# The second mixer's probability-times-value matmuls and its fold, each one pipeline step sooner

## The reference

```python
def mixer_b(h, w_in, q_gain, k_gain, cos, sin):
    z = h @ w_in                                    # three groups of q, k, v, and a gate
    for g, (window, dilation) in enumerate(((128, 1), (512, 4), (2048, 16))):
        q, k, v = ...                               # 16 query heads, 4 key heads
        q = partial_rope(rmsnorm(q, q_gain[g]), cos, sin)
        k = partial_rope(rmsnorm(k, k_gain[g]), cos, sin)
        o, lse = dilated_group(q, k, v, window, dilation)   # banded attention, keys by stride
        outs.append(o); lses.append(lse)
    wts = jax.nn.softmax(jnp.stack(lses), axis=0)   # weight of each group's result
    o = jnp.einsum('gbsh,gbshd->bshd', wts, jnp.stack(outs))
    return o.reshape(b, s, BRANCH_WIDTH) * jax.nn.silu(gate)
```

## Time and profile before

| | us |
|---|---|
| median of 3 runs | 3348.26 (3345.35 to 3348.67) |
| the profiled execution | 3348.16 |
| its span | 3346.4 |
| PE busy | 3249.7 (97%) |
| DVE busy | 2053.1 (61%) |
| ACT busy | 1642.5 (49%) |
| POOL busy | 1394.3 (42%) |

### The profile page before, as it was taken

One profiled execution on the slowest core, in us unless ns is written; L12 is line 12 of the kernel. 1 busy time (PEld: TensorE's weight loads), 2 busy tenths in 40 slices (PEclk: granted clock), 3 DMA queues, 4 the chain that ended last, 5 costly groups with the idle time before them and its releaser, 6 DMA issues. The chain is left out here.

```text
span 3346.4 us, 58949 instructions
## 1 busy us (share of the span) xinstructions
PE 3249.7 (97%) x19285; PEld 2778.4 (83%) x19285; DVE 2053.1 (61%) x4209; ACT 1642.5 (49%) x3846; POOL 1394.3 (42%) x1778
## 2 busy tenths in 40 slices
PE   8999999999999989999999999999999899999999
PEld 7887788999999977779998778888887778888887
DVE  7456773455666675548887665665347866565335
ACT  3567216667667761436665643333235743333333
POOL 6465534555667754223334344443003244443000
PEclk9999999999999989999999999999999899999999
DMA  8211772111222235200001222222464112222464
GB/s 301 80 34 47 283 272 100 47 45 51 67 67 73 76 134 188 88 26 1 0 0 51 108 76 77 91 76 91 147 222 145 68 70 81 76 91 83 147 199 162
DMA packets 111991, 338.36 MB, mean 101 GB/s; under 512 B 11794, under 2 KB 40386, under 8 KB 102979
## 3 DMA queue, kind: packets, MB, share of 16 engines
q1 hardware_dynamic: 111810, 336.12, 29.0%
HBM read 274.18 MB, written 61.10 MB: 100 GB/s over the span
## 5 line engine op out<-in xcount | busy, mean ns | idle before, releaser
L2205 PE MATMUL ps<-down_high,hidden_high 128*128 128x512 f32 x688 | 268.1, 390 | 1.1 <-DVE hidden_low L2063 0.5
L2206 PE MATMUL ps<-down_low,hidden_high 128*128 128x512 f32 x688 | 267.7, 389 | 0.0
L2207 PE MATMUL ps<-down_high,hidden_low 128*128 128x512 f32 x688 | 267.7, 389 | 0.0
L2061 DVE TENSOR_TENSOR down_low<-down_raw,down_high 128x1024 fp32r<-128x1024 f32 x86 | 108.7, 1263 | 252.1 <-ACT down_high L1970 252.0
L2141 PE MATMUL ps<-columns_combined,up_high_even 128*128 128x512 f32 (+1 forms) x648 | 247.6, 382 | 12.4 <-DVE columns_combined L4250 2.7
L2143 PE MATMUL ps<-columns_combined,up_low_even 128*128 128x512 f32 (+1 forms) x648 | 246.3, 380 | 0.0
L2142 PE MATMUL ps<-columns_combined,up_high_even 128*128 128x512 f32 (+1 forms) x648 | 246.2, 380 | 0.0
L2141 PE MATMUL ps<-columns_combined,up_high_odd 128*128 128x512 f32 x616 | 239.8, 389 | 5.4 <-DVE gates L2069 5.4
L2142 PE MATMUL ps<-columns_combined,up_high_odd 128*128 128x512 f32 x616 | 239.6, 389 | 0.0
L2143 PE MATMUL ps<-columns_combined,up_low_odd 128*128 128x512 f32 x616 | 239.6, 389 | 0.0
L1151 ACT ACTIVATE masked_then_probs<-masked_then_probs,unit_rows 128x256 f32<-128x256 f32 (+1 forms) x512 | 229.1, 450 | 21.5 <-DVE sink_term L1239 20.2
(11 more groups left out here) (473 smaller groups left out, 9777.4 us busy)
## 6 DMA issues: line engine op xcount, KB each, us to landing
mod_weights<-in_w_mod SPq DMA_DIRECT2D x48, 1024.0 KB, 6.7
up_raw<-in_w_up SPq DMA_DIRECT2D x44, 1024.0 KB, 4.8
down_raw<-in_w_down SPq DMA_DIRECT2D x88, 512.0 KB, 3.6
hidden_columns<-hidden SPq DMA_DIRECT2D x44, 512.0 KB, 2.6
hidden_columns<-hidden_columns SPq DMA_DIRECT2D x88, 256.0 KB, 3.9
w_unit_raw<-in_w_in_b SPq DMA_DIRECT2D x22, 768.0 KB, 4.4
x_kept<-x SPq DMA_DIRECT2D x24, 512.0 KB, 2.8
group_rows<-unit_rows SPq DMA_DIRECT2D x64, 132.0 KB, 1.8
```

What stands on the lines that cost most here:

```text
L2205: nc.tensor.matmul(out, h_hi[to][:, t], down_hi[to][:, cols], start=begin, stop=False)
L2206: nc.tensor.matmul(out, h_hi[to][:, t], down_lo[to][:, cols], start=False, stop=False)
L2207: last = nc.tensor.matmul(out, h_lo[to][:, t], down_hi[to][:, cols], start=False, stop=(end and to == self.slot(h, f, s)))
```

## The change

For the second mixer, out moves from step i+6 to i+5 and fold from i+7 to i+6; the first mixer keeps both. `DEPTH_` follows (6 steps of drain, not 7), and so do `FILLING` (5, not 6) and one wait of PE before it overwrites the bank that it shares with the folded columns.

```diff
-    LAG = {"project": 0, "square": 1, "scale": 2, "turn": 3, "score": 4, "turn_probs": 5, "out": 6, "fold": 7}
-    DEPTH_ = max(LAG.values())
...
+    LAG = {"project": 0, "square": 1, "scale": 2, "turn": 3, "score": 4, "turn_probs": 5, "out": 6 if SHARED else 5, "fold": 7 if SHARED else 6}
+    DEPTH_ = max(LAG.values())
...
-        FILLING = 6
+        FILLING = LAG["out"]
...
-                    elif a.g.final and not (isinstance(a.i, int) and a.i - 5 < FINAL):
-
-                        pe.wait_ge(core.turned_used.sem, core.turned_used.at(a.i - 5 - FINAL + 2))
+                    elif a.g.final and not (isinstance(a.i, int) and a.i - 4 < FINAL):
+
+                        pe.wait_ge(core.turned_used.sem, core.turned_used.at(a.i - 4 - FINAL + 2))
```

## The result

The changed kernel takes 3355.49 us (median of 11 runs, 3353.62 to 3359.57) against 3346.41 us for the kernel before (11 runs beside them, 3343.36 to 3348.67). The ratio is 1.0027, 95% interval 1.0019 to 1.0034: 9.1 us slower, 6.4 to 11.4 by the interval. In a second comparison, with other runs of the kernel before, the same changed kernel came at 1.0022 (1.0013 to 1.0031), 7.3 us slower. The profiled execution took 3356.37 us, its span is 3354.5.

What follows compares the result with a forecast made beforehand. PE, busy 637.29 of 638.00 us, bounds the steady steps; latency sets the last 28 us. Steady steps 0, work moved ahead +1.45 and drain +0.55 give +2.0 on 3348.16: 3350.2 us, 8-in-10 range 3344.5 to 3356.

Steps and rivals of the forecast that it cites:

- rival 2: Steady steps: PE meets out's wait; 0.1 us in each of 96 steps gives +9.6, 3359.8 us in all; chance 0.10.
- No change: Whole kernel: a result within about 0.2%, or 6.7 us, of the kernel before; chance 0.87.
- The steady steps: From step 7 on, the copies end before out, by 0.39 us (ACT) or 0.33 (DVE) at least; added wait priced 0.
- In the filling: Step 5 gets item 0's out; ACT's copy for it ended at 558.54, before the step's end, so no wait.
- What moves ahead of the last projection: One more out (0.62) and fold (0.36) before the last projection ends, and 0.47 more idling at step 40: +1.45 us.
- The wait at step 40: PE waits for ACT's token reordering (L1181); a short out replaces the long one in its shadow: 0.47 us more idling.
- The drain: After the last projection: +1.75 from out waiting for its own step's copy, -1.2 net from the saved step: +0.55 us.
- the clock's term: Drain step 98: out and fold take 0.98 us at full clock or 1.67 at granted 0.51; middle gives scores +1.75.
- rival 4: Drain and after: longer PE pauses bring 1.2 GHz sooner or keep it longer, +1.5 to +3, 3352.5 us; chance 0.12.
- Two of my signs: Drain: item 95's scores start 2.5 to 4 us later than 1219.98; last ACT copy ends 1 to 3 after 1232.21.
- Program order: Drain: item 95's scores stand behind the waiting out; if matmuls could pass, the drain would come to -0.8 us.
- rival 1: Drain: the saved step counts and blocked PE does not, -2.1 + 1.45 = -0.65, 3347.5 us; chance 0.13.

Runs made afterwards that it cites:

- before again: The kernel before, run and profiled a second time with no edit: 3348.90 us, ratio 1.0006.
- the kernel before with the wait: The kernel before, with PE's out in the drain also waiting for the copies of the probabilities turned in the same step: 3352.44 us, ratio 1.0016.
- filled: The kernel before, with identity turns added in PE's drain pauses, ahead of two turns of q and k and of the folds: 3348.14 us, ratio 0.9997.
- with the wait and filled: The kernel before with out's added drain wait, plus identity turns ahead of the outs and last folds: 3347.87 us, ratio 1.0000.
- lightly filled: The kernel before with fewer identity turns in its drain pauses and 12 behind the last fold: 3345.39 us, ratio 0.9994.
- the pauses filled: The changed kernel with identity turns (20, 18, 10, 10, 4) ahead of the waiting outs in the drain and 9 ahead of the last fold: 3348.14 us, 0.9997.
- the experiment with twelve more turns: The changed kernel with its drain pauses filled by identity turns, and 12 more turns behind the last fold: 3349.24 us, ratio 1.0000.

## Why the prediction was right or wrong

**The time** lies in the stated range, and the small forecast had the right direction, but not the size: +2.0 was forecast and 7.3 to 9.1 measured. That the range held it is luck in part: its upper end, 3356, had been put there for rival 2, a wait in the steady steps that did not come, and the median is 0.5 us below it. A loss beyond 0.2% had been given a chance of 0.09. The two measurements are 0.27% and 0.22%, both clear of zero, though both intervals reach below 0.2%. "No change" was wrong.

**The steady steps: right.** Out's new wait is met in all of them, by 0.40 us at the nearest where 0.39 had been read. Rival 2 fell. It was closer than I thought: in the drain PE needs 0.25 us from the end of ACT's copy to the first matmul of out, not the 0.1 I had taken for such a release. The cover is 0.15 us wide, not 0.3. (Seventeen other steps had 0.40 to 0.52 us, where I wrote some twenty.) In the filling I said no wait, and there is one of 0.90 us before the first out.

**What moves ahead of the last projection: the step holds, the size is a bit off.** Forecast +1.45. Six profiles with out at 6 (before, before again, and the kernel before with the wait, filled, with the wait and filled, and lightly filled) took 677.4 to 679.0 us for the steps, mean 678.2. Seven with the whole change took 679.7 to 680.7, mean 680.2: +2.0. The wait at step 40 was forecast as 0.70 + 0.47 = 1.17 and is 1.15. The rest can be placed by two marks, the scores of step 6 and the delayed projection at step 40. To the scores of step 6 it is +0.8 where 0.62 (item 0's out) was forecast, and this part scatters, from 32.8 to 34.5 us among the six. From there to step 40 it is +0.7 where 0.47 was forecast, and behind it +0.5 where 0.36 (one fold) was; these two repeat within 0.2 us. What the additional 0.2 and 0.15 us are is open.

**The drain: the step that failed is the clock's term in its sum, +0.55 "from -0.7 to +1.6".** Measured +4.1 and +4.9. The mechanism was right: out waits for the copy of its own step, the scores of the next item stand behind it, one step is saved. The instants were right as well, at the full clock. With the pauses filled the last item's scores come 17.37 us after the out of step 95 (1221.23 - 1203.86), 1.6 later than before where +1.4 to +2.1 was forecast; from them to the last fold it is 9.56 us, 1.3 less than before where -1.2 was. The drain is 26.93 us, +0.3 over before, inside that range. What failed is the clock. I priced it as a middle between two rates for one out and one fold in step 98. In the first profile of the changed kernel it falls at about 1216, in step 97, a step before; when it falls scatters (in the second it was step 96, and step 97 in the second profile of the kernel before). What differs in both pairs is that it stays down to the end of the drain, through all the outs, folds, scores and turns, each of which is on the chain, as PE now is in every step. That is +3.8 to +4.6 us, by the same kernel with its pauses filled. It is rival 4, for which I gave +1.5 to +3 on top of the forecast, for two more steps and a later rise, and a chance of 0.12, and which I counted as no change. Two of my signs show it: the scores of item 95 came 5.5 us later (2.5 to 4 forecast) and the last ACT copy 5.0 us later (1 to 3 forecast), both with the 3.6 us of the later start taken off. The rule of the Trainium skill ("TensorE: Matmul & The Clock Gate", Part 1), that half rate is the default and activity lifts it, had pointed here, and the trace agrees: 0.50 to 0.60 with the pauses, 1.00 with the filled ones.

**Program order: right.** In the changed drain the scores start right behind the waiting out and its fold, with no pause between (1227.38, 1228.44, 1229.06). Taken ahead of it they give back 2.4 to 3.2 us, with some of the clock's share in that. The other rule that I weighed, of the Trainium skill ("TensorE: Matmul & The Clock Gate", Part 2), is that matmuls stay in program order; the trace agrees by these three starts.

**The saved step** (rival 1) is real and worth less than what pays for it: with the wait and the filling and no saved step the drain is 28.56, with the saved step 26.93, 1.6 us where I had 2.1 at most and 1.2 net. What pays for it is the order's 1.9 to 2.4 us and the clock's 3.8 to 4.6.

**The sum** is now +2.0 in the steps and +4.5 (mean of two profiles each) in the drain, +6.5 us. The two comparisons say 9.1 (6.4 to 11.4) and 7.3 (4.4 to 10.4). Both hold it; whether the 0.8 to 2.6 us above it are real stays open. In the first pair of profiles the difference of the spans, 8.1 us, had 3.6 us of chance ahead of the mixer in it.

## What to carry to other kernels

A lag between two stages of a pipeline pays for itself outside the steady steps. Where the matmuls of the filler work are gone, in a drain, a stage that has been put into the step of its own operand stops an engine that works in fixed order, and everything queued behind it waits too. Before taking out a step of lag, walk through the drain at both levels of PE's clock. Here pauses of 3.48 and 2.71 us, where 2.10 had been the longest, went with the low level to the end of the drain, and it lengthens every piece of PE's work that the new waits have brought onto the chain. The low level cost the kernel before about 0.8 us to the last item's scores (15.8 against 15.0 us in the lightly filled one), where less of PE's work was on the chain.

## What the runs showed of the hardware that was not expected

- From the end of ACT's copy to the first of the 16 small matmuls that waited for it PE took 0.25 us, at the full clock (1214.55 to 1214.81) and at the low one (1227.13 to 1227.38) alike. Behind DVE's copy it was 0.10 where that one came last (1226.84 to 1226.94, pauses filled), and behind a single wait on POOL in the kernel before 0.05 (L957 to L1022, 1210.47 to 1210.52).
- The clock of the kernel before fell to 0.51 though none of PE's pauses had been longer than 2.10 us. Turns of a 128x128 identity in the pauses held it at 1.00; half as many let it fall to 0.66 once.
- How long the low clock lasts into the next stage differs between profiles of one kernel, and it shows. In the two of the kernel before, 19 and 10 of that stage's matmuls ran at the low rate, and the time from the last fold to the start of the stage's last matmul was 97.9 and 95.7 us. The last eight slow ones, gone in the experiment with twelve more turns, gave nothing more (94.6 and 94.7 us).
